# Two dense layers in one kernel: a compression in column groups, another order of work around the attention queries, and weight splits ahead of their turn at the opening and the last stage

## The reference, cut to what matters

```
def compress(kv_raw, pe, w1, w2):          # for keys and for values
    blocks = kv_raw[:, idx] + pe[None, None, :, None, :]
    ...
    return jax.nn.silu(blocks @ w1) @ w2   # w1 is 2048 x 256, 16 blocks x 4 groups
...
kv = (rms_norm(h, kv_norm) @ w_kv).reshape(bsz, seq, N_KV_SETS, N_KV_GROUPS, HEAD_DIM)
qg = h @ w_qg
s = jnp.einsum("bqghd,bngd->bghqn", qblk, k_cmp)        # compressed scores
o = (gblk[..., 0:1] * o_cmp + gblk[..., 1:2] * o_slc + gblk[..., 2:3] * o_win)
...
mod = jax.nn.silu(c) @ w_ada[l] + b_ada[l]              # 6 x 1024 numbers
h = modulate(rms_norm_2(x, g_mix[l]), sh_m, sc_m)       # uses the first half of mod
```

## Time and profile before

| | |
|---|---|
| median of 3 runs | 1009.28 us |
| profiled execution, its own time | 1012.89 us |
| its span | 1011.2 us |
| PE busy | 981.5 us (97%) |
| DVE busy | 709.3 us (70%) |
| ACT busy | 485.5 us (48%) |
| mean granted TensorE clock | 0.983 |

### The profile page before, as it was taken

How to read it: one execution, slowest core, us unless ns; L and a number is a source line. 1 busy time by engine, 2 the same in 40 slices (tenths; PEclk the granted TensorE clock), 3 DMA queues, 4 the chain that set the end, 5 groups by cost and what they waited for, 6 DMA issues and landing times.

```text
span 1011.2 us, 19580 instructions
## 1 busy us (share of the span) xinstructions
PE 981.5 (97%) x7974; PEld 949.9 (94%) x7974; DVE 709.3 (70%) x1138; ACT 485.5 (48%) x704; POOL 83.2 (8%) x129
## 2 busy tenths in 40 slices
PE   8799999999999998999999999999999989999998
PEld 7799999999999996779999999999999889999998
DVE  3777777777768668865777777676886577655554
ACT  4344643444446345755544444444757474444441
POOL 7000001000000012230010010002000000000000
PEclk9999999999999998979999999989999999999999
DMA  9445866877744652006667786742534365665521
GB/s 274 156 172 196 272 191 240 285 249 249 266 170 152 231 209 84 2 17 234 209 230 259 240 291 226 251 126 84 158 107 153 108 226 163 213 205 169 194 96 42
DMA packets 131389, 187.00 MB, mean 185 GB/s; under 512 B 6272, under 2 KB 102656, under 8 KB 131328
## 3 DMA queue, kind: packets, MB, share of 16 engines
q1 hardware_dynamic: 123984, 159.82, 48.0%
q0 software_dynamic: 6912, 25.17, 7.1%
q10 hardware_dynamic: 432, 1.16, 0.4%
HBM read 185.09 MB, written 1.05 MB: 184 GB/s over the span
## 4 chain that ended last, share of the span: by engine, by line
PE 82%; DVE 8%; ACT 5%; DMA 3%; issue 3%; SPq 0%; DVEq 0%; ACTq 0%
PE ps L1844 43%; PE ps L1913 15%; PE ps L1840 13%; PE ps L1842 2%; DVE g_lo L1141 2%; ACT g_hi L654 1%; DVE ada_acc L1218 1%; PE ps L2097 1%; PE ps L1880 1%; DVE g_lo L1253 1%; ACT g_hi L728 1%; DMA g_raw<-in_b_w_qg 1%; PE ps L2080 1%; DMA g_raw<-in_a_w_in 1%; DMA g_raw<-in_w_kv 1%
## 5 line engine op out<-in xcount | busy, mean ns | idle before, releaser
L1844 PE MATMUL ps<-opa_hi,g_hi 128*128 128x256 f32 x864 | 249.2, 288 | 10.9 <-DVE g_lo L1141 7.2
L1844 PE MATMUL ps<-opa_lo,g_hi 128*128 128x256 f32 x864 | 246.2, 285 | 0.0
L1844 PE MATMUL ps<-opa_hi,g_lo 128*128 128x256 f32 x864 | 246.1, 285 | 0.0
L1844 PEld LDWEIGHTS ps<-opa_hi,g_hi 128*128 128x128 f32 x864 | 167.6, 194 | 14.4 <-issue 8.7
L1253 DVE TENSOR_TENSOR g_lo<-g_raw,g_hi 128x2048 fp32r<-128x2048 f32 x54 | 123.8, 2293 | 69.8 <-ACT g_hi L728 69.8
L1844 PEld LDWEIGHTS ps<-opa_lo,g_hi 128*128 128x128 f32 x864 | 167.7, 194 | 0.1
L1844 PEld LDWEIGHTS ps<-opa_hi,g_lo 128*128 128x128 f32 x864 | 167.4, 194 | 0.0
L1141 DVE TENSOR_TENSOR g_lo<-g_raw,g_hi 128x2048 fp32r<-128x2048 f32 x57 | 130.6, 2291 | 44.8 <-ACT g_hi L654 44.2
L1913 PE MATMUL ps<-hid_hi,d_hi 128*128 128x256 f32 x528 | 147.9, 280 | 0.1
L1913 PE MATMUL ps<-hid_hi,d_lo 128*128 128x256 f32 x528 | 147.5, 279 | 0.0
L1913 PE MATMUL ps<-hid_lo,d_hi 128*128 128x256 f32 x528 | 147.3, 279 | 0.0
(11 more groups left out here) (326 smaller groups left out, 1877.5 us busy)
## 6 DMA issues: line engine op xcount, KB each, us to landing
g_raw<-in_f_w_gu SPq DMA_DIRECT2D x44, 1024.0 KB, 8.8
ada_raw<-in_w_ada POOLq DMA_DIRECT2D x48, 512.0 KB, 6.1
d_raw<-in_f_w_down SPq DMA_DIRECT2D x22, 1024.0 KB, 5.1
g_raw<-in_w_in SPq DMA_DIRECT2D x14, 1024.0 KB, 7.8
g_raw<-in_w_gate SPq DMA_DIRECT2D x11, 1024.0 KB, 7.4
g_raw<-in_w_up SPq DMA_DIRECT2D x11, 1024.0 KB, 9.8
d_raw<-in_w_down SPq DMA_DIRECT2D x11, 1024.0 KB, 5.2
g_raw<-in_a_w_in SPq DMA_DIRECT2D x10, 1024.0 KB, 7.5
```

The lines of the kernel that those rows point to most:

```text
L1844: mm = pe.matmul(pair(b)[:, a, :], wt[:, a * P:(a + 1) * P], xt, **st)
```

## The change

Four edits are made together.

1. **Opening.** CV1 is split in halves, ahead of all squares. The splits of CV2 and CV3 stand ahead of the root of the norm, and one convolution more is done before the next split.
2. **Compression, order of chunks.** The chunk of KV4 and KV5 is loaded before the first `cmp` chunk, and QG0 and QG1 before the second. `cmp_hidden(w)` now uses the 64 columns of `b_cmp` as weights and streams 256 columns of `w1`; even l go to output partitions 0 to 63, odd l to 64 to 127 (two column groups). ACT copies the sum (`tokens_copy`) into `pt_buf`, and `cmp_turn(w)` transposes it and adds the two groups with `fold`, two identities side by side, made by GpSimd. `cmp_hidden(0)` stands behind KV4, `cmp_hidden(1)` behind QG0.
3. **Modulation and query prologue.** `ada_rows` replaces the four `ada_sum` calls of the first half: 8 matmuls with 32 columns of ones as weights and 384 moving columns, in four column groups; DVE transposes the result in `make_mod(0)`, before attention begins. QG1 is done between and behind `scores(0)` and `scores(1)`. `evac_q(1)`, `compressed_shift(0)` and the splits of QG3 and WO0 move in the lists of ACT and DVE.
4. **Last stage.** The first halves of the splits of F2's first two steps are done ahead of the MO loop, and on DVE the rest of a split stands ahead of the residual.

```diff
@@ -87,11 +87,11 @@
     steps(BG, 4, False)
     steps(AO, 4, False)
     steps(F0, FT, True)
-    steps(KV, 4, False)
+    steps(KV, 6, False)
     chunks.append(("cmp", 0))
-    steps(KV + 4, 2, False)
+    steps(QG, 2, False)
     chunks.append(("cmp", 1))
-    steps(QG, 4, False)
+    steps(QG + 2, 2, False)
     steps(WO, 4, False)
     steps(F1, FT, True)
...
     vrep = gu[:, 1, :, :]
+    mod_rows = e_odd[:, 1, :]
+    fold = pt_buf[:, 0:64]
+    def hid_tok(w):
+        return pt_buf[:, 64 + 256 * w:320 + 256 * w]
     r_col = small[:, 10:12]
...
+        pool.tensor_tensor(fold, ident[:, 0:64], ident[:, 64:128], ALU.add).then_inc(fold_made, 1)
...
-        split_g(1)
-        squares(0, 2)
-        squares(0, 3)
+        act.wait_ge(g_loaded[0], 32)
+        for h, made in ((0, first_hi), (1, g_hi_made)):
+            ks = slice(4 * h, 4 * h + 4)
+            act.activation(part_view(g_hi, 1, True)[:, ks], raw_step(1)[:, ks], ACT.Copy).then_inc(made, 1)
+        for j in range(4):
+            squares(0, j)
+        split_g(CV + 2)
+        split_g(CV + 3)
         root(0)
-        split_g(CV + 2)
         for i in range(8):
             act.wait_ge(g_done, CV + i + 1)
             if i >= 2:
                 act.wait_ge(g_evac, i - 1)
             act.activation(gu[:, i % 2, 0, :], ps[:, gbank(CV + i), 0:T], ACT.Copy).then_inc(c_copied, 1)
-            if i >= 1:
...
             split_g(KV + 5)
-            act.wait_ge(cmp_hid_done, 1)
-            act.activation(hid_cmp[:, 0, :, :, :].rearrange("p a g n -> p (a g n)"), ps[:, 0, 0:128],
+            key_copies(4)
+            tokens_copy(0)
+            split_g(QG)
+            act.wait_ge(cmp_turned, 1)
+            act.activation(hid_cmp[:, 0, :, :, :].rearrange("p a g n -> p (a g n)"), ps[:, 0, 256:384],
                            ACT.Silu).then_inc(cmp_hid_silu, 1)
-            key_copies(4)
-            split_g(QG)
             split_g(QG + 1)
-            act.wait_ge(cmp_hid_done, 2)
...
+            split_g(QG + 2)
+            act.wait_ge(cmp_turned, 2)
             for a in range(2):
-                src = ps[:, 1, a * 64:(a + 1) * 64].rearrange("p (g n) -> p g n", g=NG)
+                src = ps[:, 1, 256 + a * 64:256 + (a + 1) * 64].rearrange("p (g n) -> p g n", g=NG)
                 act.activation(vrep[:, a, :].rearrange("p (g h n) -> p g h n", g=NG, h=4),
                                src.unsqueeze(2).to_broadcast([P, NG, 4, 16]), ACT.Silu).then_inc(cmp_hid_silu, 1)
...
-            n, b, at = 24 * half, (7, 3)[half], (384, 0)[half]
+            n = 24 * half
             dve.wait_ge(ada_summed, half + 1)
-            own(dve.tensor_tensor(mod[:, n:n + 24], ps[:, b, at + n:at + n + 24], par_col("b_ada_2", n, 24), ALU.add))
+            if half == 0:
+                for b in (2, 3):
+                    ins = dve.transpose(mod_rows[:, 384 * (b - 2):384 * (b - 1)], ps[:, b, 0:384])
+                ins.then_inc(ada_turned, 1)
+                dve.wait_ge(ada_turned, 1)
+                sums = mod_rows.rearrange("p (c m) -> p c m", m=32)[:, :, 0]
+            else:
+                sums = ps[:, 3, n:n + 24]
+            own(dve.tensor_tensor(mod[:, n:n + 24], sums, par_col("b_ada_2", n, 24), ALU.add))
             dve.scalar_tensor_tensor(out=gmod[:, 8 * half:8 * half + 8], in0=mod[:, n + 8:n + 16], scalar=1.0,
...
             for j in (1,) if h == 0 else (2, 3):
                 gained_lo(j, opa_hi, opa_lo, opa_hi_made, 0, opa_made, "a_norm")
-        add_squares(0, (1,))
-        split_g(1)
-        add_squares(0, (2, 3))
+        for h, hi, lo in ((0, first_hi, first_lo), (1, g_hi_made, g_lo_made)):
+            ks = slice(4 * h, 4 * h + 4)
+            dve.wait_ge(hi, 2)
+            dve.tensor_tensor(part_view(g_lo, 1, True)[:, ks], raw_step(1)[:, ks],
+                              part_view(g_hi, 1, True)[:, ks].bitcast(F32), ALU.subtract).then_inc(lo, 1)
+        add_squares(0)
+        split_g(CV + 2)
+        split_g(CV + 3)
         invert_rms(0)
         own(dve.tensor_tensor(r_sq, rstd[:, :], rstd[:, :], ALU.mult))
-        split_g(CV + 2)
         for i in range(8):
...
                 if s in (1, 2):
                     split_g(KV + s + 3)
-                if s == 3:
-                    dve.wait_ge(kv_copied, 2)
+                if s == 4:
                     dve.wait_ge(cmp_hid_done, 1)
                     cmp_blocks(1)
...
             split_g(QG + 2)
-            evac_q(1)
-            dve.wait_ge(gate_turned, 1)
-            dve.tensor_copy(gates[:, :, :], ps[:, 6, 256:352].rearrange("p (a n) -> p a n", a=TT)).then_inc(gates_copied, 1)
-            dve.wait_ge(gates_copied, 1)
+            make_mod(0)
             dve.wait_ge(kc_done, 1)
...
+            dve.wait_ge(gate_turned, 1)
+            dve.tensor_copy(gates[:, :, :], ps[:, 6, 256:352].rearrange("p (a n) -> p a n", a=TT)).then_inc(gates_copied, 1)
+            dve.wait_ge(gates_copied, 1)
+            own(dve.tensor_scalar(gates[:, :, :], gates[:, :, :], 1.0, None, ALU.add))
+            own(dve.reciprocal(gates[:, :, :], gates[:, :, :]))
...
             normalize(0)
-            normalize(1)
             shift(2)
             shift(3)
+            evac_q(1)
+            normalize(1)
+            compressed_shift(0)
+            split_g(QG + 3)
             compressed_factors(0)
             evac_q(2)
-            split_g(QG + 3)
...
                         normalize(2 * j - 2 + e)
-                    if j == 6 and e == 0:
-                        split_g(WO)
                     if j == 4 and e == 0:
                         evac_q(3)
                     if j < NH // 2:
@@ -1544,10 +1578,10 @@
                 if j == 5:
                     compressed_factors(1)
                 dve.wait_ge(opa_hi_made, 8 * A_FILL["attn"] + j - 1)
-                if j == 7:
-                    make_mod(0)
                 dve.tensor_tensor(opa_lo[:, j - 2, :], ps[:, 7, 0:T],
                                   opa_hi[:, j - 2, :].bitcast(F32), ALU.subtract).then_inc(opa_made, 1)
+                if j == 3:
+                    split_g(WO)
...
                                   ALU.subtract).then_inc(opa_made, 1)
+            for i, g in ((3, F2), (4, F2 + 1)):
+                dve.wait_ge(ahead_hi_made, i)
+                dve.tensor_tensor(part_view(g_lo, g, True)[:, 0:4], raw_step(g)[:, 0:4],
+                                  part_view(g_hi, g, True)[:, 0:4].bitcast(F32), ALU.subtract)
             for s in range(5):
+                if s < 2:
+                    split_rest(MO + s + 2)
                 if s < 4:
...
                     evac(ins, MO + s)
-                if s < 2:
-                    split_rest(MO + s + 2)
                 if s == 2:
-                    split_g(F2)
+                    split_rest(F2)
                 if s == 1:
...
-        def ada_sum(half, first=0, n=24):
...
-            for c in range(24 * half + first, 24 * half + first + n):
-                mm = pe.matmul(ps[:, b, at + c:at + c + 1], ada_acc[:, c * P:(c + 1) * P], ones[:, 0:1], start=True, stop=True)
+        def ada_rows():
+            pe.wait_ge(ada_added, 48)
+            acc = ada_acc[:, 0:3 * D].rearrange("p (c q i) -> p c q i", q=4, i=32)
+            for b in (2, 3):
+                for q in range(4):
+                    mm = pe.matmul(ps[32 * q:32 * q + 32, b, 0:384].rearrange("p (c i) -> p c i", i=32), ones[:, 0:32],
+                                   acc[:, 12 * (b - 2):12 * (b - 1), q, :], start=True, stop=True)
+            mm.then_inc(ada_summed, 1)
...
+                    q = 64 * (l % 2)
+                    mm = pe.matmul(ps[q:q + 64, w, 0:256], b_cmp[:, l, :, :].rearrange("p g n -> p (g n)"),
+                                   w1_view(c % 2)[:, l, :], start=(l < 2), stop=(l >= 14), skip_group_check=True)
+                mm.then_inc(cmp_hid_done, 1)
+            def cmp_turn(w):
+                pe.wait_ge(fold_made, 1)
+                pe.wait_ge(cmp_tok_copied, w + 1)
                 for a in range(2):
-                    for l in range(16):
-                        mm = pe.matmul(ps[:, w, a * 64:(a + 1) * 64], w1_view(c % 2)[:, l, a * P:(a + 1) * P],
-                                       b_cmp[:, l, :, :].rearrange("p g n -> p (g n)"), start=(l == 0), stop=(l == 15))
-                mm.then_inc(cmp_hid_done, 1)
+                    mm = pe.matmul(ps[:, w, 256 + 64 * a:320 + 64 * a], hid_tok(w)[:, a * P:(a + 1) * P], fold,
+                                   start=True, stop=True, skip_group_check=True)
+                mm.then_inc(cmp_turned, 1)
             for s in range(6):
...
                     mm.then_inc(r_turned, 1)
-                if s in (3, 5):
-                    cmp_hidden((s - 3) // 2)
+                if s == 4:
+                    cmp_hidden(0)
...
             g_step(QG, opb_hi, opb_lo, filled(opb_made, B_FILL["b"]))
+            cmp_hidden(1)
             pe.wait_ge(side_lo, 2)
...
             mm.then_inc(gate_done, 1)
```

(18 more changed lines are left out.)

## The result

The changed kernel takes 1000.11 us in the median of 5 runs (996.88 to 1001.55), against 1009.28 before; the ratio is 0.9902, with a 95% interval of 0.9883 to 0.9920. That is 9.2 us less, where 13.3 had been forecast. 1000.11 lies just above the forecast's own range (993 to 1000) and inside the range that was to hold 8 in 10 (990 to 1003.5); of the named times, rival A's 1002 is nearer to it than 996. The profiled execution is one of these runs, with 1000.11 us itself and a span of 998.4. One later run of the kernel before, in the last group of experiments, took 5343 us and is left out of every figure.

What follows compares the result with a forecast made beforehand. PE was taken as the bound, busy 981.5 of 1011.2 us. Terms -6.1 - 6.6 - 0.9 = -13.6 took the profiled 1012.89 to 999.3 and the median 1009.28 to 995.7, said as 996; range 993 to 1000, 8-in-10 range 990 to 1003.5.

Steps and rivals of the forecast that it cites:

- rival A: Prologue takes back attention's gain: late load +2, slower transposes +1, lower clock +3.5 us; time 1002, chance 0.18.
- The opening: Start of the kernel: earlier splits let CV4 start at 38.6 instead of 45.6; less half a lower-clock cost, -6.1 us.
- The compression: KV and QG stage: overlapping column groups make each compression 3.8 us instead of 7.26, saving PE 6.0 in both.
- the new wait ahead of KV4: KV4 loses the compression that hid its split: PE waits 4.0 us, with the lower clock behind it.
- rival B: Column groups do not overlap for these shapes: compression 6.9 us, `ada_rows` 5.1; time 1004, chance 0.07.
- The prologue: QG0 to `values(0)`: gives nothing by itself; `values(0)` starts at 393.8, 0.9 us later than before.
- Attention: `values(0)` to `values(7)`: PE loses four `ada_sum`, DVE a wait and a split; 7.6 us shorter, 2.5 of lower clock included.
- DVE is the one that PE waits for from pair 4 on: Attention: from pair 4 DVE sets the pace, 6.1 us a pair against 5.1 of PE.
- Last stage: F2: early split halves let its second step start at 822.2 instead of 823.20; -0.9 us, between -1.7 and +0.3.
- the median, 3.6 lower: Whole kernel: the sum applied to the profiled 1012.89 gives 999.3; the median, 3.6 lower, goes from 1009.28 to 995.7.
- the middle: KV0 to `values(7)`, compression, prologue and attention together: net -6.6 us, with bounds of -11 and -1.
- D: Slower: PE stays at 1.2 GHz from `scores(0)` to `values(7)` and becomes the bound; 1015 to 1030 us, chance 0.05.

Runs made afterwards that it cites:

- opening_alone: The kernel before with only the opening edit added: 1005.60 us, ratio 0.9942.
- wo0_back: The changed kernel with WO0's split back between the normalizations of pair 6 on DVE and behind pair 5 on ACT: 1003.91 us, ratio 0.9946.
- last_alone: The kernel before with only the last-stage edit added: 1008.40 us, ratio 0.9979.
- filled_wait: The changed kernel with 15 matmuls of ones, whose result nobody reads, ahead of KV4: 1001.19 us, ratio 0.9924.
- kv_splits_first: The changed kernel with KV4's split ahead of KV1's evacuation and pad_copies(1), and KV5's ahead of key_copies(2): 995.89 us, ratio 0.9870.
- ada_sums_back: The changed kernel with the first half's modulation sums again in values(2) to values(5), no ada_rows or prologue transposes: 1000.32 us, ratio 0.9926.

## Why the forecast was right, and where it was too large

**The opening (-6.1; alone 5.9 us by the ratios and 3.8 by the medians, KV0 4 to 5 us earlier in the traces).** Right in mechanism and order: opening_alone has the waits of about 1 and 2.3 us and CV4 at 38.87, for 38.6. The size was somewhat too large. The 45.6 that it counts from is ACT's copy, and CV4 itself began near 45.3; and from CV4 to KV0 opening_alone takes 1.4 us more than before, with a lower clock behind CV4, for which the forecast had taken 0.85. In the changed kernel's profiled execution the lower clock came at CV0 as well.

**The compression (3.8 us; 3.67) and the new wait ahead of KV4 (4.0; 4.06).** Right, and worked out from rows of before. The column groups overlap, so rival B is out. "QG0 starts 4.3 earlier" is what the milestones show, -4.3.

**The prologue (`values(0)` 0.9 later from KV0; 3.7 later).** This is the first term that was mis-sized. The forecast had QG2's chunk issued 5.0 us after QG0 and landed 7.6 later; this row shows it issued 4.5 after QG0, and ACT's split of it starts at 364.44, 9.4 later:

```profile
355.04 0.95 SPq L478 DMA_DIRECT2D g_raw<-in_b_w_qg  x2
```

ACT's activations stand behind that split, and "PE waits 1.5 to 2 us in pieces" was 2.25 at one place. DVE's transposes took 1.04 us as forecast, and PE waits at most 0.78 us for them in any kept trace. For the lower clock, 0.52 from 367 to 374, the walk had nothing; seven us at that grant cost up to some 3.4 us, an estimate from the row. That is enough for what is left of the 2.7 to 2.8 us.

**Attention (-7.6; -10.7).** The mechanism was right in its main part: DVE's list is on the path, and wo0_back shows 3.0 to 3.5 us for the one split. But "DVE is the one that PE waits for from pair 4 on" does not hold as it stands, since ACT ended 3.5 us of PE's waits and DVE 2.1. The lower clock that was added (2.5 us) did not come in this execution; it came in others with the same attention code, with 50.35 to 51.45 us instead of 49.80. "PE loses four `ada_sum`" was worth 1.5 us in the trace and nothing that the time shows, since PE has idle time there. The other side of the difference is before's execution: beside opening_alone's 57.09 us the gain is 7.3 and not 10.7.

**Last stage (-0.9; -1.8 by the trace; alone 2.1 by the ratios, 1.0 by the medians).** The first gap is 0.68, as forecast under 1, and the kernel is 0.6 us shorter behind F2, which the forecast had nearly left out.

**What made the forecast too large** is, as far as the runs tell, the step "the median, 3.6 lower": the sum -13.6 was made on an execution of 1012.89 us at a mean clock of 0.983, and taken from a median of 1009.28. The part that falls short is the middle: 6.6 us forecast, 4.0 (2.7 to 5.5) measured alone. The 38 runs of before in the three groups have these clocks, among others: 18 have 0.988, with 1008.84 us in the mean; 8 have 0.984 or 0.985, with 1010.96; 5 have 0.989, with 1006.98; none has 0.983. The profiled one thus had more half-rate time than any of them. By the mean grants, some 18 us of it lay in attention (0.15 x 2 x 60.5 us), where opening_alone, with the same work, had 10 (0.09 x 2 x 57.1). The opening had some of it too: behind the same wait at CV1 (2.02 and 2.01 us) the grant from 20 to 25 us was 0.79 in before and 1.00 in last_alone, whose KV0 comes 1.7 us earlier. So a part of the forecast removed stretches that a typical run does not have. But the long stretch in attention was no single accident: last_alone repeats it, 60.46 us at 0.85. By the runs at 0.988 on both sides, 1008.84 before and 1000.11 and 998.49 after, the change gave 8.7 and 10.4 us. How often the old attention runs at 0.85 and how often at 0.91 or above, three traces cannot tell, and no second profile of the kernel before was taken. So where the missing 3.6 to 4 us lie is argued and not shown.

Rival A names what took place in kind, a prologue that gives back: QG2's load took 1.8 us longer than walked, and the lower clock was there, though not in attention in this execution. Its 1002 is 1.9 us off and the forecast's 996 is 4.1, so on the time alone A did better. D is out: it needed the lower clock all through attention, and no trace of the new attention has a mean grant under 0.93.

## What to carry to other kernels

A sum that is made on one profiled execution holds for that execution. Before it is taken from a median, compare the mean granted clock of the two, and leave out what the change would take from half-rate stretches that a typical run does not have. Before PE's work is made shorter, look whether PE or the chain split, load, split sets the next start. Filling PE's wait with work that nobody needs tells the two apart: if the next start does not move, it is the chain. Here halving the two compressions gave some 2 us, while splitting KV4 and KV5 ahead of the copies gave 3 to 4, and putting the ready work of the gates into the wait for the load, together with one split's better place, 2 to 3.5. A split belongs where its engine is idle anyway: the same 2.29 us cost 3.0 to 3.8 us more in pair 6 than at the end of pair 3.

## What the runs showed of the hardware

The lower clock followed PE's longer waits. All seven profiled executions with the 4.05 to 4.06 us wait ahead of KV4 have a mean grant of 0.93 to 0.96 between KV0 and QG0. In filled_wait, 15 matmuls without a use in that wait kept it at 1.00, and the next wait of 3.59 us, which was not filled, was followed by a mean of 0.66 over 5 us. But it is not a fixed price of a wait. Opening_alone waited 2.33 us ahead of CV4 and kv_splits_first 2.36; in the 6.2 us behind that wait the mean grant was 0.72 in one, with 39 matmuls, and 1.00 in the other, with 52. The changed kernel idles 5.6 us in short pieces in attention with a grant of 1.00 all through.

The mean clock of a run varies from 0.984 to 0.991 for one and the same kernel (38 runs of before), and its time mostly goes with it, by 0.7 us for each 0.001 on a line through all 38 and 0.9 between two of their groups (1010.96 us at 0.984 to 0.985, 1006.98 at 0.989). It is no measure by itself: two runs of ada_sums_back show 0.938 and 0.941 with 1002.51 and 1000.17 us, beside 1004.82 at 0.983.

Two STREAM_TRANSPOSE of 384 float32 columns took 1.04 us on DVE, and 8 float32 matmuls of 384 moving columns in four column groups of 32 took 1.50 us.
